# The front of a query tile: steps in another order, three banks in turn, and the next tile's norms in its middle

## What is computed

```python
z = h @ p["w_in"][l]
zq, zkv, zkr, rq, rk, rv, rg, sq, sk, sv = jnp.split(z, splits, axis=-1)
q = (rmsnorm(zq, p["g_q_norm"][l]) @ p["w_uq"][l]).reshape(B, L, MLA_HEADS, MLA_NOPE + MLA_ROPE)
latent = rmsnorm(zkv, p["g_kv_norm"][l])
k_rope = rope(zkr, pos)
rq = rope(rq.reshape(B, L, RET_HEADS, RET_DK), pos) * (RET_DK ** -0.5)
rk = rope(rk.reshape(B, L, RET_HEADS, RET_DK), pos)
kv = (lat_all @ p["w_ukv"][l]).reshape(B, -1, MLA_HEADS, MLA_NOPE + MLA_V)
# A: softmax attention, 8 heads, over k_nope, k_rope and v of kv
# B: retention, 4 heads: decayed q k^T v, plus a state carried from chunk to chunk, group norm, silu(rg) gate
# C: stick-breaking attention, 4 heads, over sq, sk, sv
mix = jnp.concatenate([mla_out, ret_out, sb_out], axis=-1) @ p["w_o"][l]
```

## Time and profile before

| | |
|---|---|
| Time before, median of 3 runs | 1782.06 us (1781.98 to 1783.7) |
| The profiled execution | 1783.8 us |
| its span | 1782.1 us |
| PE busy in the span | 1671.7 us (94%) |
| DVE, ACT, POOL busy | 1060.8, 645.0, 179.6 us (60, 36, 10%) |
| PE work in the chain that ended last | 85% of the span |
| HBM traffic | 107.54 MB read, 27.29 MB written |

### The profile page before, as it was taken

The page is one execution under the profiler, slowest core; times in us unless marked ns, Lnnn a source line. Parts: engine busy times, 40 slices in busy tenths (PEclk is TensorE's granted clock), DMA queues, the critical chain, the costliest instruction groups (busy, mean ns, idle before and its releaser), DMA issues.

```text
span 1782.1 us, 27943 instructions
## 1 busy us (share of the span) xinstructions
PE 1671.7 (94%) x10051; PEld 1498.6 (84%) x10051; DVE 1060.8 (60%) x2269; ACT 645.0 (36%) x1252; POOL 179.6 (10%) x235
## 2 busy tenths in 40 slices
PE   6699999989788999999998999999999999999996
PEld 3499999835556677777898999999999999999996
DVE  5843333237687766767525666666666666666657
ACT  7522211225555656667424422221222122212213
POOL 0011111122333212311120000000000000000000
PEclk9899999978889999999999999999999999999999
DMA  9264444431121101005410111111111111111003
GB/s 347 81 233 153 137 129 141 136 108 37 40 92 47 43 16 47 4 13 173 148 48 13 48 48 60 36 47 35 59 35 47 35 59 35 47 35 59 12 1 113
DMA packets 114423, 133.63 MB, mean 75 GB/s; under 512 B 15003, under 2 KB 91722, under 8 KB 113002
## 3 DMA queue, kind: packets, MB, share of 16 engines
q1 hardware_dynamic: 110953, 121.83, 21.2%
q0 software_dynamic: 3328, 10.73, 1.7%
q10 hardware_dynamic: 64, 0.07, 0.0%
HBM read 107.54 MB, written 27.29 MB: 76 GB/s over the span
## 4 chain that ended last, share of the span: by engine, by line
PE 85%; DVE 7%; ACT 4%; issue 3%; DMA 1%; SPq 0%; DVEq 0%; ACTq 0%; POOLq 0%
PE psum L2002 33%; PE psum L2066 15%; PE psum L1783 13%; PE psum L1971 5%; PE psum L1924 3%; PE psum L1868 2%; PE psum L1953 2%; PE psum L1928 2%; PE psum L1822 1%; PE psum L1817 1%; PE psum L1718 1%; PE psum L1849 1%; PE psum L1719 1%; DVE h_lo L1356 1%; DVE act_lo L1356 1%
## 5 line engine op out<-in xcount | busy, mean ns | idle before, releaser
L2002 PE MATMUL psum<-act_hi,wt_parts 128*128 128x362 f32 (+1 forms) x2496 | 615.6, 328 | 9.5 <-DVE act_lo L1356 5.2
L1655 DVE SCALAR_TENSOR_TENSOR residual<-psum,mod,residual 128x364 f32<-128x364 f32 (+2 forms) x704 | 299.8, 496 | 257.6 <-PE psum L2066 257.6
L2002 PEld LDWEIGHTS psum<-act_hi,wt_parts 128*128 128x128 f32 x2496 | 442.3, 189 | 12.2 <-issue 6.8
L2002 PE MATMUL psum<-act_lo,wt_parts 128*128 128x362 f32 (+1 forms) x1248 | 409.0, 328 | 0.0
L2066 PE MATMUL psum<-u_hi,wt_parts 128*128 128x362 f32 (+1 forms) x1056 | 263.3, 331 | 3.0 <-issue 3.0
L2002 PEld LDWEIGHTS psum<-act_lo,wt_parts 128*128 128x128 f32 x1248 | 235.6, 189 | 0.0
L2066 PEld LDWEIGHTS psum<-u_hi,wt_parts 128*128 128x128 f32 x1056 | 188.1, 189 | 3.3 <-issue 3.3
L1783 PE MATMUL psum<-w_hi,h_hi 128*128 128x308 f32 (+1 forms) x576 | 177.6, 308 | 12.1 <-DVE h_lo L1356 10.9
L1783 PE MATMUL psum<-w_lo,h_hi 128*128 128x308 f32 (+1 forms) x576 | 177.0, 307 | 0.0
L1783 PE MATMUL psum<-w_hi,h_lo 128*128 128x308 f32 (+1 forms) x576 | 176.5, 306 | 0.0
L2066 PE MATMUL psum<-u_lo,wt_parts 128*128 128x364 f32 (+1 forms) x528 | 174.7, 331 | 0.0
(11 more groups left out here) (222 smaller groups left out, 2289.3 us busy)
## 6 DMA issues: line engine op xcount, KB each, us to landing
wt_raw<-in_w_up SPq DMA_DIRECT2D x44, 512.0 KB, 3.8
ada_raw<-in_w_ada SPq DMA_DIRECT2D x32, 512.0 KB, 4.1
wt_raw<-in_w_down SPq DMA_DIRECT2D x22, 512.0 KB, 4.3
w_raw<-in_w_in SPq DMA_DIRECT2D x16, 616.0 KB, 6.9
z_scratch<-z_out POOLq DMA_DIRECT2D x64, 154.0 KB, 2.3
z_in<-z_scratch SPq DMA_DIRECT2D x8, 1232.0 KB, 5.3
ada_first<-in_w_ada SPq DMA_DIRECT2D x16, 512.0 KB, 11.5
xT_scratch<-xT SPq DMA_DIRECT2D x1, 4352.0 KB, 15.6
```

Of the source, the lines that this page charges most:

```text
L1655: last = dve.scalar_tensor_tensor(out=res[:, d, a:b], in0=bank[4 + q % 4][:, a - CHUNKS[c][0]:b - CHUNKS[c][0]], scalar=mod[:, 40 + d, whi ...
L2002: last = pe.matmul(out[:, :b - a], ww[:, slot, P * k:P * k + P], aa[:, k, a:b], start=(k == 0 and m == 0), stop=(k == KT - 1 and m == 2))
```

## The change

The steps of a front get an order of their own: position `p` of the front does step `FRONT[p]`, which is 0, 1, 4, 9, 2, 3, 10, 5, 6, 7, 8, 11. The fronts of tiles 2 to 5 write banks 1, 3 and 7 in turn (their neighbours' units have at most 512 keys, so banks 1 and 3 are free), and so do positions 6 to 11 of tile 0 with banks 2, 3 and 7; all others stay in bank 7. Before a step PE waits for the readers of the last user of its own bank, and besides for the datum that the step needs. The preparation of a tile (norms, `zqn`, `lat`, rotations) is done at position 6 of the front before, and for tile 0 ahead of the loop; the product `kd` stays at position 0 and gets a semaphore of its own. The amount of computation is the same.

```diff
+FRONT = [0, 1, 4, 9, 2, 3, 10, 5, 6, 7, 8, 11]
+AT = {what: p for p, what in enumerate(FRONT)}
+PREP_AT = 6
+def front_bank(m, p):
+    if 2 <= m <= 5:
+        return (1, 3, 7)[p % 3]
+    if m == 0 and p >= 6:
+        return (2, 3, 7)[p % 3]
+    return 7
+def bank_user_before(m, p):
+    for q in range(12 * m + p - 1, -1, -1):
+        if front_bank(*divmod(q, 12)) == front_bank(m, p):
+            return divmod(q, 12)
+    return None
...
 # POOL
+            def prepare(m):
+                r, slot = rows_of(m), m % 2
+                pool.wait_ge(s_zi[slot], 48 * (m // 2 + 1))
+                if m:
+                    pool.wait_ge(s_latst, 32 * m)
+                    pool.wait_ge(s_fp, 12 * (m - 1) + AT[9] + 1)
...
+                if p == PREP_AT and m + 1 < NTILE:
+                    prepare(m + 1)
...
 # ACT: squares, Ln and Exp in prepare(m), called at PREP_AT before the step's own copy
-                act.wait_ge(s_fp, 12 * m + s + 1)
+                act.wait_ge(s_fp, 12 * m + p + 1)
...
 # DVE
+            def prepare(m):
+                dve.wait_ge(s_rs, m + 1)
+                if m:
+                    dve.wait_ge(s_fp, 12 * (m - 1) + max(AT[1], AT[4]) + 1)
+                    dve.wait_ge(s_latst, 32 * m)
+                dve.tensor_scalar(zqn[:r], ...)
+                dve.scalar_tensor_tensor(out=lat[:r], ...).then_inc(s_lat, 1)
...
 # PE
+            def front_emptied(m, p):
+                pe.wait_ge(s_fA, read_a(m, p + 1))
+                pe.wait_ge(s_fD, read_d(m, p + 1))
...
-                    pe.wait_ge(s_fA, read_a(m, s))
-                    pe.wait_ge(s_fD, read_d(m, s))
+                if bank_user_before(m, p):
+                    front_emptied(*bank_user_before(m, p))
+                if m == 0 and p == 6:
+                    pe.wait_ge(s_cA, 6)
+                    pe.wait_ge(s_cD, 5)
...
                 elif s in (5, 6):
+                    front_emptied(m, AT[s - 3])
...
                 elif s == 11:
+                    pe.wait_ge(s_kd, m + 1)
+                    pe.wait_ge(s_fD, read_d(m, max(AT[9], AT[10]) + 1))
...
 # PE, scores(i)
+                if i % 12 == 0:
+                    front_emptied(n, AT[7])
+                if i % 12 == 1:
+                    front_emptied(n, AT[8])
```

More of the change, by code:

```diff
@@ L212, with read_a, read_d @@
 PV_NO = {i: v for v, i in enumerate(PV_ORDER)}
[L214 to L224, removed]
+FRONT = [0, 1, 4, 9, 2, 3, 10, 5, 6, 7, 8, 11]
+AT = {what: p for p, what in enumerate(FRONT)}
+READ_A = {0, 1, 2, 3, 4, 5, 7, 8, 9}
+READ_D = {0, 2, 3, 4, 6, 7, 9, 10, 11}
+PREP_AT = 6
+def read_a(m, p):
+    return len(READ_A) * m + sum(x in READ_A for x in FRONT[:p])
+def read_d(m, p):
+    return len(READ_D) * m + sum(x in READ_D for x in FRONT[:p])
+def front_bank(m, p):
[9 more added lines that the diff above has]
+    return None
 def build(nc, I, O, stop_after=None):
@@ L817, in stick_exponents @@
                     .then_inc(s_wa, 1)
+            prepare(0)
             for step in range(-12, STEPS):
@@ L1008, in cache_copy, with front @@
                     act.activation(v_mla[:, 4:6, :], psum[:, 4:6, :], ACT.Copy).then_inc(s_cA, 1)
-            def front(m, s):
+            def prepare(m):
                 r, slot = rows_of(m), m % 2
-                b7, col = bank[7], key_col(m)
                 x = z_in[:r, slot, :]
[L1015 to L1024, removed]
+                act.wait_ge(s_zi[slot], 48 * (m // 2 + 1))
+                if m:
+                    act.wait_ge(s_lat, m)
+                act.activation(junk[:r, :QR], x[:, O_ZQ:O_ZQ + QR], ACT.Square, scale=QR ** -0.5,
+                               accum_out=sums[:r, 0:1])
+                ch.link(act.activation(junk[:r, QR:], x[:, O_KV:O_KV + KVR], ACT.Square, scale=KVR ** -0.5,
+                                       accum_out=sums[:r, 1:2]))
+                ch.link(act.activation(rs[:r], sums[:r], ACT.Ln, bias=eps[:r]))
+                act.activation(rs[:r], rs[:r], ACT.Exp, scale=-0.5).then_inc(s_rs, 1)
+            def front(m, p):
+                r, slot, s = rows_of(m), m % 2, FRONT[p]
+                b7, col = bank[front_bank(m, p)], key_col(m)
+                x = z_in[:r, slot, :]
+                if p == 0:
                     if m:
@@ L1429, in cache_copy, with prepare, front @@
                     dve.tensor_copy(v_mla[:, 6:8, :], psum[:, 0:2, :]).then_inc(s_cD, 1)
-            def front(m, s):
+            def prepare(m):
                 r, slot = rows_of(m), m % 2
-                b7, col = bank[7], key_col(m)
-                v4 = b7.rearrange("p (k n) -> p k n", k=4)
[L1435 to L1444, removed]
+                x = z_in[:r, slot, :]
+                dve.wait_ge(s_rs, m + 1)
+                if m:
+                    dve.wait_ge(s_fp, 12 * (m - 1) + max(AT[1], AT[4]) + 1)
+                    dve.wait_ge(s_latst, 32 * m)
+                dve.tensor_scalar(zqn[:r], x[:, O_ZQ:O_ZQ + QR], rs[:r, 0:1], None, ALU.mult)
+                dve.scalar_tensor_tensor(out=lat[:r], in0=x[:, O_KV:O_KV + KVR], scalar=rs[:r, 1:2],
+                                         in1=g_kv[:r], op0=ALU.mult, op1=ALU.mult).then_inc(s_lat, 1)
+            def front(m, p):
+                r, slot, s = rows_of(m), m % 2, FRONT[p]
+                b7, col = bank[front_bank(m, p)], key_col(m)
+                v4 = b7.rearrange("p (k n) -> p k n", k=4)
+                if p == PREP_AT and m + 1 < NTILE:
+                    prepare(m + 1)
+                if p == 1:
                     dve.wait_ge(s_g1, m + 1)
@@ L1458, in tab @@
                         return rope_t[:r, slot, 128 + a:128 + a + n].unsqueeze(1).broadcast_to([r, 4, n])
-                    if not (m == 0 and s == 2):
-                        dve.wait_ge(s_fD, read_d(m, s))
+                    dve.wait_ge(s_fD, read_d(m, p))
                     dve.tensor_tensor(q_a[:r], q4[:, :, NOPE:QD], tab(0, ROPE), ALU.mult)
@@ L1841, in cache_step, with front @@
                     last.then_inc(s_cT, 1)
-            def front(m, s):
-                r, slot, b7 = rows_of(m), m % 2, bank[7]
+            def front_emptied(m, p):
+                pe.wait_ge(s_fA, read_a(m, p + 1))
+                pe.wait_ge(s_fD, read_d(m, p + 1))
+            def front(m, p):
+                r, slot, b7, s = rows_of(m), m % 2, bank[front_bank(m, p)], FRONT[p]
                 x = z_in[:r, slot, :]
```

40 lines of the change are left out of this document (23 added, 17 removed).

## The result

The changed kernel takes 1771.99 us (median of four runs, 1767.99 to 1774.02) against 1782.66 for the kernel before on the same chip: a ratio of 0.9937, 95% interval 0.9918 to 0.9955. It is faster by 0.6%, 11 us, where 40 were forecast and 1725 to 1766 was the range. The profiled execution took 1767.99 us (span 1766.3), the shortest of the four: the two profiled spans differ by 15.8 us, the medians by 11.

| tile | 0 | 1 | 2 | 3 | 4 | 5 | 6 | 7 |
|---|---|---|---|---|---|---|---|---|
| before | 41.8 | 46.1 | 38.3 | 36.7 | 42.2 | 48.0 | 55.7 | 60.2 |
| after | 37.9 | 48.4 | 33.8 | 40.7 | 44.7 | 45.7 | 50.8 | 56.0 |

A forecast was written before the change was run, and what follows sets the result against it. Bound taken: PE's waits, chiefly for DVE's `skT` copy at tile starts, plus a slow clock. Gains 20.7 + 6 + 12 + 10 less 9 given back make 40 us: 1742 on the median's basis, range 1725 to 1766.

The forecast's parts named there:

- (a): Tile starts: preparation moved to the front before removes PE's waits for `skT` in tiles 2 to 8, 20.7 us.
- Rival E: One-bank tiles: `skT` stays behind the retention output, so only 25 us are gained, 1757; chance 0.05.
- (b): Order and waits per datum, tiles 2 to 5: PE stops waiting for the one bank's last reader, 6 us gained.
- the paragraph on what hides the moved work in the middle: At position 6, PE's step of 2.2 to 3.9 us covers the moved work; POOL's share costs nothing.
- (e): Given back: 6 us at head outputs in tiles 2 to 5 and 3 us for eight middles.
- Its own signs of being wrong: Slow stretches still there, head outputs taking over the gaps, or a 3 us gap opening at position 7.
- The 1751: Time if PE waited for all the 1.1 us moved, not removed, in eight middles: 31 us gained instead of 40.
- (c): Clock after tile 1's start: without idle time, stretches mostly stay at full clock, 12 us gained (bounds 0 and 16.7).
- (d): Tile 0 and tile 1's start: three banks from position 6 cut waits and clock loss, 10 us gained.
- C: DVE sets the pace: tiles 2 to 5 give nothing, only 9.2 us of tiles 6 to 8 remain, 1773; chance 0.07.
- D: The middle becomes the new stall: eight middles cost 50 us, so the kernel is slower, 1792; chance 0.06.
- B: Idle time goes but the clock still falls as PE runs ahead in bursts: 23 us gained, 1759; chance 0.12.

The follow-up runs named there:

- old_order_squares_earlier: old_order_banks with ScalarE's squares, Ln and Exp for the next tile moved from position 6 to directly behind position 5: 1746.0 us, ratio 0.9783.
- squares_earlier: Changed kernel with GpSimd's rotations at position 10 instead of 6 and ScalarE's squares behind position 5 instead of at 6: 1752.9 us, ratio 0.9821.
- one_bank: Changed kernel with bank 7 alone for every front step, instead of banks in turn: 1786.3 us, ratio 1.0020.
- old_order_banks: Changed kernel with the old order of steps 0 to 11 and GpSimd's rotations at position 10; banks in turn stay: 1748.9 us, ratio 0.9805.
- products_first: Changed kernel with GpSimd's rotations at position 10 and the two `w_uq` product steps back at positions 2 and 3: 1752.1 us, ratio 0.9816.

## Why the prediction was wrong

**What held.** (a) at the starts: `oc` is at 425 ns in every tile, the waits for `skT` are gone, and the one-bank tiles 6 to 8 gained 12.1 us with the clock at 1.00, where 9.2 of wait and some clock were forecast. Rival E is out. (b) as far as the bank goes: in tiles 2 to 5 no front step waits. Preparation and banks together, where the order is left alone, gave 35 us, and 39 with ACT's squares a position earlier (old_order_squares_earlier): nearly all of the 40 was there to be had. One reading was off without harm: in the earlier trace rows `mixtok` ran beside `kd`, not beside a rotation. `kd` now ends before `oc` starts (609.49 and 611.55 in tile 6), and `mixtok` too took the 0.42 us that (a) gave it (416 to 427 ns).

**The step that failed first** is the paragraph on what hides the moved work in the middle, and with it the 3 us for the middles and the 6 for head outputs in (e). It laid PE's step of 2.2 to 3.9 us over the whole chain and charged 0.4 us a tile. In tile 3 the chain from ACT's first square (500.48) to the end of the head output (506.12) is 5.6 us: 1.6 on ACT, 2.3 for `zqn` and `lat`, 1.7 for `att`, the row maximum and the head output behind them. PE had 2.5 us of work beside it and stood 3.2. In tiles 2 to 5 these waits make 10.0 us, and those at the starts grew by 9.0 where (e) put 6. Taking away the two delays of the middle (squares_earlier) gave 21 us by the ratios. Between the profiled executions it is 14.6, of which 14.3 in tiles 2 to 5, 1.8 to 5.7 each. Three things were missed. DVE waits for `rs` 13.3 us in seven middles, since ACT starts the squares only behind position 6's piece copy. `zqn` and `lat` run beside the rotation, which was seen; but the "nothing" for POOL counted POOL's own waiting and not what its place does to DVE, 12 us. And `weigh` waits for the head output one unit back, which is queued on DVE behind norms, `att` and a row maximum. The prediction named that queue and then did not sum it. Its own signs of being wrong came: slow stretches were left, head outputs took over the gaps, and gaps of 3.0 and 3.2 us opened in the middles of tiles 2 and 3, a step later than it said.

The Trainium skill, page "SBUF — State Buffer", section "Who interferes with whom", lets the later of DVE and GpSimd block on the shared ports. The trace agrees: `lat` took 1.49 us beside the rotation, ending 0.28 us behind it, and 0.48 without. The 1751 worked out from it was too kind, since the delay cost more than its length at position 6 and nothing at position 10.

**The second** is (b): order and waits were booked as one gain of 6 us. The order costs 7 or 11 us by itself, with one bank or three. That it puts the long products two positions later, behind small transposes, was not weighed at all.

**(c)** was mis-sized: 58.6 us of PE work at half clock became 49.2, which by the same 45% is 4 us instead of 17 (12 and the 5 in (d)). The clock from 414 to 716 us was 0.95, not 0.97. In tiles 2 to 4 it stayed down behind the gaps, and in tile 1 for 17.1 us in which PE was busy for 15.8. **(d)** was half right: the front of tile 0 ends 5.6 us earlier (its last product at 394.3 against 399.8), 1.6 of it because it began earlier, but tile 1 lost 2.3 us of that with its clock at 0.50 until 415.7.

**The rivals.** C came nearest with 1773, and its picture is right (tiles 2 to 5 gave 0.3 us). Its cause isn't, in the middles, since a move of DVE's instructions undoes the waits there; of the 12.2 us at the starts, that move left 11.0. D named the mechanism and over-priced it: it put 6.2 us on each of eight middles, and they cost 1.8 to 5.7 in tiles 2 to 5 and 0.7 or less in tiles 6 and 7, which have more work on PE. B's clock did fall in tiles 2 to 4, but behind those stalls. The Trainium skill, page "TensorE: Matmul & The Clock Gate", section "A second HAM failure mode: psum-queue depth-cycling", tells of a kernel whose clock went up and down in small gaps while it turned through banks. Here turning banks gained 12 to 16 us in all three pairs of kernels that differ by it alone, and the time at half clock from 384 us on fell each time (75 to 51 us, 61 to 48, 48 to 27), so the measurement speaks against it.

From before, in steps: preparation -19, banks -16, order +11, rotations at 6 +12. That these end at the -11 measured, but for rounding, proves nothing, as each step starts where the last one ended.

## What to carry to other kernels

Moved work is covered only up to the next hand-back that the busy engine waits for: follow the receiving queue to that instruction, and sum what stands ahead of it. Where a producer on another engine feeds the moved work, put the producer a step earlier (14 us here), and keep work of a third engine that lengthens the moved instructions out of that step (12 us). When one diff holds a reorder, more buffers and a move, cost and test each alone: here two gained 35 us and the third, with what it made possible, took 23 back.

## What the hardware showed

Beside a rotation on POOL, DVE's `lat` took up to 1.51 us against 0.48 and `zqn` up to 1.44 against 0.41; the same collision cost 12 us at one position, 6 there once another delay was gone, and nothing clear of noise at another position. The clock, once down to 0.50 early in tile 1, stayed there for 17.1 us in after and 20.5 in one_bank, and for 6.8 us in old_order_banks, whose first long products come two positions earlier. Their place doesn't settle it alone: in products_first, with the long products early too, the clock was down for 24.0 us, from 386.4 in tile 0 into tile 1.
